# Delta rule's output normed and turned by token halves, and memory tokens loaded behind it

## What is computed

```python
def deltanet_mixer(h, w_in, conv_w, a_log, dt_bias, norm_g, w_out):
    ...
    o = gated_delta_rule_chunked(q, k, v, beta, g)      # 8 heads of 128, chunks of 64
    o = o * lax.rsqrt(jnp.mean(o * o, axis=-1, keepdims=True) + RMS_EPS) * norm_g
    o = o * jax.nn.silu(z).reshape(b, s, DN_HEADS, DN_HEAD_DIM)
    return o.reshape(b, s, kd) @ w_out                  # 256x1024 @ 1024x1024

# second block
    mh = rmsnorm_2(mem, g_mem_norm[l])                  # 256 memory tokens of 1024
    mkv = jnp.einsum('bmd,de->bme', mh, w_mem_kv[l])
```

## Time and profile before

| | |
|---|---|
| median of three runs | 1947.37 us |
| the profiled execution | 1951.39 us |
| its span | 1949.6 us |
| mean granted clock of TensorE | 0.993 |
| TensorE busy | 1897.9 us |
| VectorE, ScalarE, GpSimd busy | 1448.9, 1227.2, 72.3 us |
| HBM traffic | 267 GB/s over the span |

### The profile page before, as it was taken

One profiled execution on the slowest core, in us unless ns is written; L12 is line 12 of the kernel. 1 busy time (PEld: TensorE's weight loads), 2 busy tenths in 40 slices (PEclk: granted clock), 3 DMA queues, 4 the chain that ended last, 5 costly groups with the idle time before them and its releaser, 6 DMA issues.

```text
span 1949.6 us, 26960 instructions
## 1 busy us (share of the span) xinstructions
PE 1897.9 (97%) x9904; PEld 1567.8 (80%) x9904; DVE 1448.9 (74%) x1263; ACT 1227.2 (63%) x1074; POOL 72.3 (4%) x107
## 2 busy tenths in 40 slices
PE   7999999898999999999999999999999999899999
PEld 6888877786788888888888888888878778788887
DVE  5654656665798898988989888898997656676554
ACT  5544556423677777778777787877777357645442
POOL 0000000000100000000000000000401100000000
PEclk9999999998999999999999999999999999999999
DMA  7974634002699999999999999999995432255552
GB/s 305 366 293 146 223 122 172 2 3 97 263 395 365 399 376 369 405 370 389 365 380 389 361 407 364 388 382 366 389 351 194 174 129 87 91 179 184 194 181 79
DMA packets 76638, 521.12 MB, mean 267 GB/s; under 512 B 8208, under 2 KB 8464, under 8 KB 17296
## 3 DMA queue, kind: packets, MB, share of 16 engines
q1 hardware_dynamic: 72224, 503.27, 67.1%
q0 software_dynamic: 4192, 16.25, 2.1%
q10 hardware_dynamic: 144, 0.52, 0.1%
HBM read 501.14 MB, written 18.87 MB: 267 GB/s over the span
## 4 chain that ended last, share of the span: by engine, by line
PE 75%; DVE 5%; ACT 3%; issue 2%; POOL 1%; DVEq 0%; ACTq 0%; POOLq 0%
PE bank L868 15%; PE bank L863 15%; PE bank L864 15%; PE bank L524 7%; PE bank L525 7%; PE bank L541 7%; PE bank L721 1%; PE bank L885 1%; PE bank L597 1%; ACT w_hi L1334 1%; DVE w_lo L2267 1%; DVE w_lo L1921 1%; DVE kT L2001 0%; PE bank L675 0%; POOL small L1816 0%
## 5 line engine op out<-in xcount | busy, mean ns | idle before, releaser
L2267 DVE TENSOR_TENSOR w_lo<-raw,w_hi 128x2048 fp32r<-128x2048 f32 x336 | 761.8, 2288 | 106.0 <-ACT w_hi L1518 101.7
L1518 ACT ACTIVATE w_hi<-raw 128x2048 fp32r<-128x2048 f32 x336 | 643.1, 1919 | 146.2 <-PE bank L868 146.1
L1921 DVE TENSOR_TENSOR w_lo<-raw,w_hi 128x2048 fp32r<-128x2048 f32 (+2 forms) x136 | 297.6, 2197 | 161.9 <-ACT w_hi L1334 160.7
L1334 ACT ACTIVATE w_hi<-raw 128x2048 fp32r<-128x2048 f32 (+2 forms) x136 | 249.3, 1840 | 167.6 <-PE bank L541 160.4
L863 PE MATMUL bank<-w_hi,xT 128*128 128x512 f32 x896 | 353.7, 395 | 0.0
L864 PE MATMUL bank<-w_hi,xT 128*128 128x512 f32 x896 | 349.2, 390 | 0.0
L524 PE MATMUL bank<-w_hi,xT 128*128 128x512 f32 (+1 forms) x784 | 311.0, 398 | 16.9 <-DVE xT L2601 7.6
L525 PE MATMUL bank<-w_hi,xT 128*128 128x512 f32 (+1 forms) x784 | 305.2, 391 | 0.0
L868 PE MATMUL bank<-w_lo,xT 128*128 128x512 f32 x896 | 240.3, 390 | 0.7 <-DVE w_lo L2267 0.6
L868 PEld LDWEIGHTS bank<-w_lo,xT 128*128 128x128 f32 x896 | 168.0, 188 | 37.2 <-DVE w_lo L2267 2.0
L864 PEld LDWEIGHTS bank<-w_hi,xT 128*128 128x128 f32 x896 | 168.4, 188 | 33.8
(11 more groups left out here) (438 smaller groups left out, 1839.0 us busy)
## 6 DMA issues: line engine op xcount, KB each, us to landing
raw<-in_experts_dram SPq DMA_DIRECT2D x336, 1024.0 KB, 6.9
raw<-in_tiles_dram SPq DMA_DIRECT2D x125, 1024.0 KB, 4.8
rows_in<-zeros POOLq DMA_DIRECT2D x1, 6144.0 KB, 32.7
rows_out<-zeros POOLq DMA_DIRECT2D x1, 5632.0 KB, 55.2
raw<-in_tiles_dram SPq DMA_DIRECT2D x9, 512.0 KB, 3.3
item_rows<-rows_in SPq DMA_DIRECT2D x7, 512.0 KB, 7.3
rows_out<-y_s SPq DMA_DIRECT2D x7, 512.0 KB, 3.8
row<-in_rows_dram SPq DMA_DIRECT2D x1, 1040.0 KB, 14.9
```

The source lines that it names most:

```text
L1334: nc.scalar.activation(w_hi[:, i % SPL, 0:kc * w], raw[:, i % DENSE, 0:kc * w], ACT.Copy)\
L1518: nc.scalar.activation(w_hi[:, w_slot(j), :], raw[:, raw_slot(j), :], ACT.Copy).then_inc(m_hi, 1)
L1921: nc.vector.tensor_tensor(w_lo[:, i % SPL, 0:kc * w], raw[:, i % DENSE, 0:kc * w], w_hi[:, i % SPL, 0:kc * w], ALU.subtract).then_inc(spli ...
L2267: nc.vector.tensor_tensor(w_lo[:, s, :], raw[:, raw_slot(j), :], w_hi[:, s, :], ALU.subtract).then_inc(m_lo, 1)
```

## The change

- The second-half buffers of the delta rule move from the low-part slots to the spare `raw` slots; VectorE waits for the zero rows' transfer first, since the zeros lie there.
- VectorE makes the low part of the first `dn_out` tile in the first half's part of the scan, ScalarE the high part of the third in the same place.
- ScalarE squares each head by itself, with the sum in the same instruction; VectorE's two reductions go. GpSimd takes the root of each token half by itself.
- VectorE gates half 0 before the second half of the scan, for which it waits for eight squares, and scales half 0 before it adds half 1's output. Half 1 is gated after the scan and scaled by groups of four heads.
- TensorE's filler products go. It transposes half 0 (two banks of four blocks), does tiles (0, 0) and (1, 0) with half 0, transposes half 1, does tile (0, 1) with half 0 and then all three with half 1. High and low activations are made 128x512 at a time.
- SP loads the memory tokens after the last `dn_out` tile, when half 1 has been scaled; ScalarE squares them after the transposed activations, GpSimd takes the root after the delta rule's.

```diff
-                                                         offset=low_parts + 2048 * (6 * _h + _i))
+                                                         offset=spare + 2048 * (6 * _h + _i))
...
 # TensorE, tile_parts
+                if by_token:
+                    for tt in range(NT):
+                        for half in range(k0 // KC, (k0 + kc - 1) // KC + 1):
+                            result((by_token, tt, half))
+                        high_products(tt)
+                        pe.wait_ge(split_lo, i + 1)
+                        last = low_products(tt)
+                        if tt == 0:
+                            yield
+                    last.then_inc(used, 1)
+                    return
...
 # TensorE, end of the delta rule
-                keep_busy(10)
-                pe.wait_ge(xn_done, 2)
-                turn_norm("o", xn)
+                def turn_o(tt, half):
+                    pe.wait_ge(o_normed, 2 + half if tt else 1)
+                    b = tp_bank(("turned o", tt, half), "D")
+                    for k in range(KC):
+                        ch = KC * half + k
+                        last = nc.tensor.transpose(b[:, k * P:k * P + P], xn[:, tt, ch * P:ch * P + P], ident)
+                    last.then_inc(tp_done, 1)
+
+                turn_o(0, 0)
+                turn_o(0, 1)
                 out0, out1 = ("dn_out", 0), ("dn_out", 1)
                 begin(out0, "D")
-                tile(out0, 0, xT1, xT2, turned="o")
                 begin(out1, "D")
-                tile(out1, 0, xT1, xT2)
-                tile(out0, 1, xT1, xT2, turned="o")
+                parts = [tile_parts(name, j, xT1, xT2, by_token="turned o") for name, j in ((out0, 0), (out1, 0), (out0, 1))]
+                next(parts[0])
+                next(parts[1])
+                turn_o(1, 0)
+                turn_o(1, 1)
+                next(parts[2])
+                for part in parts:
+                    next(part, None)
...
 # SP
-            load(range(6, cbs["gate", 1, 0][0]))
+            load(range(6, cbs["dn_out", 1][1]))
+            sp.wait_ge(o_normed, 3)
             sp.dma_start(mem_in[:, :, :], t["mem_2"][0].rearrange("(t p) d -> p t d", p=P)).then_inc(mem_loaded, 16)
-            load(range(cbs["gate", 1, 0][0], NA))
+            load(range(cbs["dn_out", 1][1], NA))
+
+            sp.wait_ge(sq_done, squares_done("mm"))
...
 # ScalarE, for each token half of the scan
-                    act.wait_ge(o_done, 2 * tt + 2)
-                    tell(nc.scalar.activation(o_sq[tt][:, :], xn[:, tt, :], ACT.Square), o_squared)
-                norm_turn("o", "dn_norm", 0)
+                    for hg in range(2):
+                        act.wait_ge(o_done, 2 * tt + hg + 1)
+                        for hh in range(4 * hg, 4 * hg + 4):
+                            cols = slice(hh * P, hh * P + P)
+                            tell(nc.scalar.activation(o_sq[tt][:, cols], xn[:, tt, cols], ACT.Square,
+                                                      accum_out=dnv[:, V_SS, 8 * tt + hh:8 * tt + hh + 1]), o_squared)
+                    if tt == 0:
+                        split_to(cbs["dn_out", 0][1])
+                for tt in range(NT):
+                    for half in range(2):
+                        tell(nc.scalar.activation(xT1[:, KC * half:KC * half + KC, tt * P:tt * P + P],
+                                                  batch(("turned o", tt, half))[:, :].rearrange("p (a b) -> p a b", a=KC), ACT.Copy,
+                                                  scale=G("dn_norm")), hi_out)
+                act.wait_ge(mem_loaded, 16)
+                norm_squares("mm", mem_in, mem_junk[:, :])
...
 # GpSimd
-            norm_root("mm")
...
-            pool.wait_ge(small_dve, 5)
-            tell(inverse_root(dnv[:, V_R, :], dnv[:, V_SS, :], dnv[:, V_TMP, :]), rs_ready)
+            for tt in range(NT):
+                pool.wait_ge(o_squared, 2 + HEADS * (tt + 1))
+                y, v, u = (dnv[:, q, 8 * tt:8 * tt + 8] for q in (V_R, V_SS, V_TMP))
+                own(nc.gpsimd.tensor_scalar(v, v, 1.0 / P, EPS, ALU.mult, ALU.add))
+                tell(inverse_root(y, v, u), rs_ready)
+            norm_root("mm")
...
 # VectorE, in the scan's loop over tt
                     if tt:
-                        head_sums(0)
-                        own(nc.vector.tensor_tensor(xn[:, 0, :], xn[:, 0, :], z_s[:, 0, :], ALU.mult))
+                        dve.wait_ge(rs_ready, 2)
+                        o_scaled(0)
+                    else:
+                        state["limit"] = NA
+                        split_to(cbs["dn_out", 0][0] + 1)
...
+                    if tt == 0:
+                        dve.wait_ge(o_squared, 2 + HEADS)
+                        o_gated(0)
+                dve.wait_ge(o_squared, 2 + 2 * HEADS)
+                o_gated(1)
+                o_low(0, 0)
+                o_low(0, 1)
+                split_to(cbs["dn_out", 0][0] + 2)
+                dve.wait_ge(rs_ready, 3)
+                o_scaled(1, 0)
+                o_scaled(1, 1)
+                split_to(cbs["dn_out", 0][0] + 3)
+                o_low(1, 0)
+                o_low(1, 1)
                 add_to_h(("dn_out", 0), 0)
```

More of the change, by code:

```diff
@@ L190, in build @@
         w_hi = sb("w_hi", [P, SPL, KC * CB], FR)
-        low_parts = nc.sbuf_base
         w_lo = sb("w_lo", [P, SPL, KC * CB], FR)
@@ L317, in build @@
         acc, tp = bank[:4], bank[4:]
-        NORMS = ("n0", "n1", "mm", "n2", "n3", "m2", "fin", "m3")
+        NORMS = ("n0", "n1", "n2", "mm", "n3", "m2", "fin", "m3")
         HALVED = ("n3", "m2", "fin")
@@ L392, in build @@
         xn_done = sem("xn_done")
+        o_normed = sem("o_normed")
         norm_ready = sem("norm_ready")
@@ L505, in begin, with tile_parts @@
                 group_of[name] = (acc[2 * (g % 2):2 * (g % 2) + 2], cbs[name][1], owner, groups.count(owner))
-            def tile_parts(name, j, a1, a2, turned=None, ready=None):
+            def tile_parts(name, j, a1, a2, turned=None, ready=None, by_token=None):
                 banks, n, tiles = group_of[name][0], cbs[name][2], tiles_of[name]
@@ L525, in high_products, with low_products @@
                         nc.tensor.matmul(o, x2, b1, start=False, stop=False)
-                pe.wait_ge(split_hi, i + 1)
+                def low_products(tt):
+                    for k in range(kc):
+                        b2 = w_lo[:, s, k * n:k * n + n]
+                        x1 = a1[:, k0 + k, tt * P:tt * P + P]
+                        last = nc.tensor.matmul(banks[tt][:, 0:n], x1, b2, start=False,
+                                                stop=j == len(tiles) - 1 and k == kc - 1)
+                    return last
+                pe.wait_ge(split_hi, i + 1)
+                if by_token:
[9 more added lines that the diff above has]
+                    return
                 if turned:
@@ L838, in experts @@
                 tile(mv, 0, xT1, xT2, turned="mm")
-                pe.wait_ge(xn_done, 4)
+                pe.wait_ge(xn_done, 2)
                 pe.wait_ge(picked0, 2)
@@ L1110, in second_block @@
                         if (br, c) == (0, 1):
-                            turn_norm("mg", xn, (0,), (xn_done, 5))
+                            turn_norm("mg", xn, (0,), (xn_done, 3))
                         gemm(("branch", br, c), "D", oT1[br], oT2[br])
@@ L1115, in second_block @@
                 tile(out0, 0, xT1, xT2, turned="mg")
-                turn_norm("mg", xn, (1,), (xn_done, 5, 6))
+                turn_norm("mg", xn, (1,), (xn_done, 3, 4))
                 begin(out1, "D")
@@ L1536, in experts @@
                 first_split(0)
-                act.wait_ge(xn_done, 4)
+                act.wait_ge(xn_done, 2)
                 memory_block("mk", [k_raw[:, tt * CB:tt * CB + CB] for tt in range(NT)])
@@ L2052, in deltanet @@
                 dve.wait_ge(small_act, 2)
+                dve.wait_ge(rows_zero, 32)
                 def by_token(v, tt, hg):
@@ L2094, in deltanet, with o_heads, o_gated, o_scaled @@
                     level(1, tt)
[L2095 to L2099, removed]
+                def o_heads(tt, hg=None):
+                    return (slice(0, HEADS) if hg is None else slice(4 * hg, 4 * hg + 4),
+                            xn[:, tt, :] if hg is None else xn[:, tt, hg * CB:hg * CB + CB])
+                def o_gated(tt):
+                    own(nc.vector.tensor_tensor(xn[:, tt, :], xn[:, tt, :], z_s[:, tt, :], ALU.mult))
+                def o_scaled(tt, hg=None):
+                    now, o = o_heads(tt, hg)
+                    n = now.stop - now.start
+                    o = o.rearrange("p (a b) -> p a b", a=n)
+                    tell(nc.vector.tensor_tensor(o, o, dnv[:, V_R, 8 * tt + now.start:8 * tt + now.stop].unsqueeze(2)
+                                                 .broadcast_to((P, n, P)), ALU.mult), o_normed)
+                def o_low(tt, half):
+                    b = batch_of["turned o", tt, half][0]
```

(6 more changed lines are left out.)

5 lines of the change are left out of this document (1 added, 4 removed).

## The result

| | before | changed |
|---|---|---|
| median | 1951.63 us (20 runs) | 1953.61 us (20 runs) |
| ratio, with its 95% interval | | 1.0018 (1.0010 to 1.0026) |
| the profiled execution, span | 1949.6 us | 1951.6 us |
| transposes of h after the last product group with the state | 45.80 us | 47.87 us |

The change costs some 3.5 us by the ratio, 2.0 by the medians; both lie inside the 0.2% that I called the least that can be told, and with twenty runs the sign is clear. The last row is a length that I use all through: from the start of the last product group with the state (433.29 in the earlier trace rows) to the start of the transposes of h (479.09). It leaves out what the clock did earlier in an execution, and I call it the stage. It scatters too: a second execution of the kernel before has 43.42, 2.4 less, because its projection starts at full clock.

The account below looks back on a forecast made before the run. TensorE, busy 97% of the span, bounds the kernel. Scan loses 4.4 and 2.4, scan to projection gains 10.7, transposes cost 0.9, the add's wait 1.2: 1.8 to 1.9 us faster, median 1945.5, range 1941.0 to 1949.8.

Parts of the forecast that it names:

- The wait in the scan: Before the second half's right sides, VectorE waits for eight squares (0.42 us each) and gates: 4.4 us late, TensorE gap 4.75.
- Rival 2: Sixteen per-head squares on the path are dear: no faster at 0.54 us each, 3.2 us slower at 0.74; chance 0.14.
- The clock in that gap: TensorE's 4.75 us gap before the second half's new values very likely takes the clock down: 2.4 us lost.
- The bound of 7.7: Upper bound on clock loss after the scan's gap: all 7.7 us of following work at half clock, 7.7 more.
- From scan to projection: Last scan product to first projection product: 16.1 us becomes 5.4, a gain of 10.7.
- The projection: Three tiles, 72 products: 16.4 us plus 2.4 at low clock plus 0.9 for second-half transposes, ending at 474.3.
- What is late next: VectorE makes the fifth tile's low part before adding to h, so TensorE waits 1.2 us at the transposes of h.
- Memory tokens: Load moved behind the second scaling, squares and root following: costs nothing, with 0.4 us to spare.
- The rule on transposes: Transposes do not count as TensorE activity for the clock; if they did, 2.4 us more gained at the projection's start.

Follow-up runs that it names:

- the variant with the add first: Changed kernel with first-half gate behind the second half's right sides, and first column block added to h before the fifth tile's low part: ratio to before 0.9949, 1940.67 us.

## Why the prediction was wrong

Both ends failed: the sign, and the range (1941.0 to 1949.8 against 1953.61). The measured median lies 8.1 us above the forecast of 1945.5. Half of that is the base: I applied the difference to a median of three that lay 4.3 us under that of twenty. On the base of twenty the forecast would have been 1949.8 and the range 1945.3 to 1954.1, with the measured median in it; the sign was wrong all the same.

By its own steps, in the pair of profiled executions, less the 1.60 us that the changed one was late at the last product with the state:

| | forecast | measured |
|---|---|---|
| new values of the second half start | +4.4 | 440.83 - 434.70 - 1.60 = +4.5 |
| scan ends | +6.8 | 454.02 - 442.37 - 1.60 = +10.1 |
| first projection product | -3.9 | 459.23 - 458.46 - 1.60 = -0.8 |
| transposes of h | -1.8 | 482.76 - 479.09 - 1.60 = +2.1 |

Of the 3.9 us between forecast and measured in the last row, the clock in the scan's gap is 3.1 (5.5 against 2.4); the rest is in the smaller terms below. Against the second execution of before, whose stage is 2.4 shorter, the last row would be +4.4. The first two rows do not hang on which of the two is taken: its scan takes 7.7 us as well.

- *The wait in the scan*: right in mechanism and size. A square of 128 columns with its sum repeats after 0.43 us (0.42 forecast), eight of them and the gate hold the right sides back by 4.5 us. Rival 2, dear squares, is refuted; the kernel became slower at 0.43.
- *The clock in that gap* is the step that failed. I took 2.4 us, half of a low stretch of 4.8, from the row at 458.46, where full-width products follow the gap. With the scan's products behind the gap it did not come back before the scan ended: 5.5 us lost where I had 2.4. The bound of 7.7 was in the sum; the choice between the ends went by the wrong neighbour. No row showed the scan's products behind a gap. The case stood as one sentence inside rival 2, and should have been a rival of its own with a larger chance. The other term of its kind, 2.4 lost at the projection's start in both kernels, held for the pair compared here; in the second execution of before nothing is lost there. Nor was a long gap as sure to take the clock down as I had it: in the execution shown first the projection product at 277.61 comes after an idle stretch of 2.82 us at full clock (0.47), in the second the same one, at 281.46 after 2.83, at the lower (0.77).
- *From scan to projection*: 5.2 us against 5.4, right. GpSimd's root took 6.0 and not 4.0 (457.13 to 463.11), and VectorE waited 0.94 for it, within the 3.4 us of cover.
- *The projection*: 20.1 against 19.7; the low clock at its start lasted 0.8 us longer (to 465.1, where before it was to 463.5).
- *What is late next*: the fifth tile's low part ahead of the add was named and mis-sized by little, 1.47 against 1.2, and the variant with the add first shows the cause: there the wait is gone.
- *Memory tokens*: nothing, as forecast, in the changed kernel (loaded 464.6, landed in 4.8, squared from 469.68 without a wait). The thin cover was real: 2.81 us of wait appeared when the projection ran faster.
- *The rule on transposes* (the Trainium skill, TensorE: Matmul & The Clock Gate, Part 4: PE-mode transpose) changed nothing in the sum: in the changed kernel the clock came back at 454.8, with the first half's transposes, behind the scan's output products, and was gone again when the projection began. But my "the row agrees" rested on one execution. In the second one of before the clock came back within 461 to 462 while TensorE had run only transposes since 458.68, so the rule does not hold there, and the measurement decides: transposes left the clock down in one execution and brought it back in the other.

## What to carry to other kernels

A wait put into a chain of matmuls that has run without one can cost twice: its own length, and a stretch at 1.2 GHz behind it. What that stretch costs is to be read where the same products follow a gap, not where others do; in this scan it was more than the wait. Before moving work of a side chain ahead of the chain that ends last, ask whether it could stand behind that chain's next link for nothing, as the gate could. Take a base from more than three runs when the forecast is of the size of their scatter. And read a clock effect from more than one execution: the same stop took the clock down in one and left it up in another.

## What the runs showed of the hardware

- After stops of 1.93, 3.19, 4.46 and 4.88 us in the scan the clock fell and stayed at 1.2 GHz for 10.2 to 13.7 us, until 3.4 to 5.0 us after the 128x128 output products had begun. Four full-width filler products had it back after 4.2 us. The Trainium skill (TensorE: Matmul & The Clock Gate, Part 1: The HAM clock gate) ties the clock to how busy TensorE has been; in 446 to 450 of the changed kernel the clock stood at 0.50 with TensorE shown busy for 4.00 of 4.00 us.
- Products of 64x64 of the array at 390 us had the clock back after 3.4 us at 1.2 GHz in one execution and 6.8 in another, and transposes alone had it back within 461 to 462 in the second execution of before.
- The kernel before has low stretches at 28, 52, 281, 366 and 390 us in one execution and at 317 alone in another. A stop of 1.85 us left the clock up in one of them and took it down in the other.
- On GpSimd operations on 128x8 that take 0.20 us elsewhere took 1.23 (457.13) and 2.10 (460.16) beside VectorE's gate (457.07 to 458.30) and low part (459.91 to 462.20), operations with two inputs from SBUF. The Trainium skill (GPSIMD Engine Reference, 8. Key points) states contention in that case; the rows agree and give the size: each ended within 0.1 us of VectorE's instruction.
